# A hybrid decoder step: six query tiles multiplied as three pairs, decoding moved behind them

## What is computed

```python
def split_projection(h, w_in):
    z = jnp.einsum('bsd,de->bse', h, w_in)
    ...
    qd, kd, vd, gd, qw, kw, vw, gw, qm, gm = jnp.split(z, cuts, axis=-1)
    qd = qd.reshape(B, S, H_DIFF, 2, DK_DIFF)
...
    od = diff_attn_prompt(qd, kd, vd, lam, slopes_diff)
    ow = dilated_prompt(qw, kw, vw, slopes_dil)
    om = memory_attn(qm, mk, mv)
    yp = yp + gated_merge(od, gd, ow, gw, om, gm, g_subln[l], lam_init, w_out[l], yp.dtype)
...
    od = diff_attn_sample(qd, kd, vd, cache_k_diff[l], cache_v_diff[l], page_table, lam, slopes_diff)
```

## Time and profile before

| | |
|---|---|
| median of 3 runs | 1026.35 us (1026.08 to 1027.72) |
| the profiled execution's own time | 1026.25 us |
| its span, first to last instruction | 1024.5 us |
| PE busy | 1000.5 us, 98% |
| DVE busy | 723.7 us, 71% |
| ACT busy | 441.5 us, 43% |
| mean granted clock of TensorE | 0.997 of full speed |

### The profile page before, as it was taken

One profiled execution on the slowest core, in us unless ns is written; L12 is line 12 of the kernel. 1 busy time (PEld: TensorE's weight loads), 2 busy tenths in 40 slices (PEclk: granted clock), 3 DMA queues, 4 the chain that ended last, 5 costly groups with the idle time before them and its releaser, 6 DMA issues.

```text
span 1024.5 us, 24055 instructions
## 1 busy us (share of the span) xinstructions
PE 1000.5 (98%) x8103; PEld 980.4 (96%) x8103; DVE 723.7 (71%) x2687; ACT 441.5 (43%) x1169; POOL 54.7 (5%) x122
## 2 busy tenths in 40 slices
PE   7999999999999999999999999999999999999995
PEld 6899999999999999999999999999999999999995
DVE  5783267777788867778777676577774786588874
ACT  5763222222333333444342553335565365545552
POOL 0200000000000000000000000000000100000002
PEclk9999999999999999999999999999999999999998
DMA  9863288987978877777866686999662425234424
GB/s 300 250 195 107 64 266 265 293 271 226 266 220 254 259 231 235 219 224 207 245 200 192 186 249 181 231 280 284 193 191 72 140 74 153 94 104 145 124 84 167
DMA packets 254521, 203.33 MB, mean 198 GB/s; under 512 B 12480, under 2 KB 207670, under 8 KB 253750
## 3 DMA queue, kind: packets, MB, share of 16 engines
q1 hardware_dynamic: 253934, 200.67, 65.7%
q10 hardware_dynamic: 464, 1.12, 0.3%
HBM read 189.98 MB, written 11.76 MB: 197 GB/s over the span
## 4 chain that ended last, share of the span: by engine, by line
PE 91%; DVE 2%; ACT 2%; issue 2%; SPq 1%; DMA 1%; POOL 0%; DVEq 0%; POOLq 0%; ACTq 0%
PE z L1097 71%; PE z L1123 8%; PE o_ps L1193 2%; PE s_ps L1156 2%; PE t_ps L1143 2%; PE t_ps L1183 1%; PE s_ps L1161 1%; DMA w_raw<-in_w_mem_kv_dram 1%; PE o_ps L1198 1%; PE o_ps L1202 1%; PE s_ps L1168 1%; PE o_ps L1242 1%; ACT w_hi L1351 1%; PE s_ps L1028 1%; SPq L828 1%
## 5 line engine op out<-in xcount | busy, mean ns | idle before, releaser
L1097 PE MATMUL z<-act_hi,w_hi 128*128 128x260 f32 (+1 forms) x2048 | 440.9, 291 | 2.4 <-DVE act_lo L1629 2.3
L1097 PE MATMUL z<-act_hi,w_lo 128*128 128x260 f32 (+1 forms) x2048 | 422.4, 283 | 0.0
L1097 PE MATMUL z<-act_lo,w_hi 128*128 128x260 f32 (+1 forms) x2048 | 421.6, 282 | 0.0
L1097 PEld LDWEIGHTS z<-act_hi,w_hi 128*128 128x128 f32 x2048 | 321.5, 189 | 7.9 <-issue 4.0
L1097 PEld LDWEIGHTS z<-act_lo,w_hi 128*128 128x128 f32 x2048 | 319.9, 188 | 0.0
L1097 PEld LDWEIGHTS z<-act_hi,w_lo 128*128 128x128 f32 x2048 | 319.5, 188 | 0.0
L1676 DVE TENSOR_TENSOR w_lo<-w_raw,w_hi 128x512 fp32r<-128x512 f32 x302 | 206.8, 687 | 132.5 <-ACT w_hi L1351 131.8
L1351 ACT ACTIVATE w_hi<-w_raw 128x512 fp32r<-128x512 f32 x302 | 186.4, 626 | 200.4 <-PE z L1097 173.2
L1865 DVE CUSTOM_DVE_ANT_0 pages<-pages,q_bc 128x128 f32<-128x128 f32 x640 | 144.2, 285 | 21.2 <-DMA pages<-in_cache_k_win_dram 13.5
L1894 DVE SCALAR_TENSOR_TENSOR v_acc<-pages,dec_a,v_acc 128x256 f32<-128x256 f32 x224 | 94.3, 478 | 1.7 <-DMA pages<-in_cache_v_diff_dram 1.5
L1473 ACT ACTIVATE probs<-probs,st_n 128x128 f32<-128x128 f32 (+3 forms) x48 | 26.8, 558 | 79.9 <-DVE st_n L1804 79.6
(11 more groups left out here) (236 smaller groups left out, 1121.8 us busy)
## 6 DMA issues: line engine op xcount, KB each, us to landing
w_raw<-in_w_in_dram SPq DMA_DIRECT2D x224, 256.0 KB, 4.5
pages<-in_cache_k_diff_dram SPq DMA_DIRECT2D x128, 256.0 KB, 4.7
pages<-in_cache_v_diff_dram SPq DMA_DIRECT2D x128, 256.0 KB, 3.6
w_raw<-in_w_out_dram SPq DMA_DIRECT2D x64, 256.0 KB, 2.8
w_raw<-in_w_mem_kv_dram SPq DMA_DIRECT2D x32, 256.0 KB, 6.1
cat<-in_x_prompt_dram SPq DMA_DIRECT2D x8, 1024.0 KB, 6.0
q_bc<-q_rows_dram SPq DMA_DIRECT2D x32, 256.0 KB, 6.7
pages<-in_cache_mem_k_dram SPq DMA_DIRECT2D x16, 256.0 KB, 6.4
```

Source lines behind the costliest of these rows:

```text
L1097: last = nc.tensor.matmul(zb[:, bank, 0:b - a], lhs[:, w], rhs[:, kt, a:b], start=(kt == 0 and m == 0), stop=(kt == KT - 1 and m == 2))
```

## The change

Of the eight `qd` tiles the first two stay single tiles (ops 32 to 39), and the other six become three pairs (ops 40 to 81). The operands T1 to T4 of the tokens are made for them in the same `arena` as those of the output pairs. For that the tokens are first added up again from their high and low parts (`token_sum`, 16 instructions of 128x520), then `operand_add` makes T1 to T4 (8 groups of four instructions of 128x260), then they are split (8 times 128x1040 on ACT and on DVE). Since `arena` also holds pages, bias tables and keys, decoding begins four slots after the last pair instead of after the fourth query tile, and ends four slots later than before (slot 256 and on); its 320 units are spread over fewer slots. The operand sums of the output pairs, of which six groups stood ahead of the output tiles, now all stand behind their start. The sample columns of all eight query tiles are kept by one instruction behind the pairs.

```diff
@@ units
-        paired = kind == "y" and c == 0 and FIRST_PAIRED <= e <= LAST_PAIRED
+        paired = kind == "qd" and e >= SINGLE_HEADS or kind == "y" and c == 0 and FIRST_PAIRED <= e <= LAST_PAIRED
@@
+Q_PAIRS = H - SINGLE_HEADS
+Q_END = START[PAIRS_OF_TILES[Q_PAIRS - 1]] + 14
@@
-T_ADDS = ((2, -11), (0, -10), (1, -9), (4, -8), (5, -7), (3, -4), (6, 1), (7, 1))
+T_ADDS = ((2, 1), (0, 1), (1, 2), (4, 2), (5, 3), (3, 3), (6, 4), (7, 4))
 T_SPLITS = ((2, 0), (1, 0), (2, 1), (1, 1), (3, 0), (3, 1), (4, 0), (4, 1))
-T_SPLIT_AT = (-4, 2, 2, 3, 4, 4, 6, 8)
+T_SPLIT_AT = (5, 6, 7, 8, 9, 10, 11, 12)
...
+X_SUM_AT = tuple(IN_START + 1 + j // 2 for j in range(HALF_KT))
+X_ADD_AT = tuple(IN_START + 4 + 5 * j // 8 for j in range(HALF_KT))
+X_SPLIT_AT = tuple(IN_START + t for t in (9, 9, 10, 10, 11, 12, 14, 16))
@@ plan
-    first, end = DONE[AT["qd", 1, 1]] + 4, DONE[AT["gw", 3, 0]] - 2
+    first, end = Q_END + 4, DONE[AT["gw", 3, 0]] + 2
@@ product
-                    if k == 0:
-                        pe.wait_ge(s_tlo, T_SPLITS.index((t, i)) + 1)
+                    if k in (0, Q_PAIRS):
+                        pe.wait_ge(s_tlo, len(T_SPLITS) * (k // Q_PAIRS) + T_SPLITS.index((t, i)) + 1)
@@ operand_hi
-                act.wait_ge(s_tadd, T_ADDED[half])
+                act.wait_ge(s_tadd, HALF_KT + T_ADDED[half] if again else HALF_KT)
@@ vector
+            def token_sum(j):
+
+                dve.wait_ge(s_plo, 3 * N_PREP)
+                dve.wait_ge(s_xsl, 1)
+                for i in range(2):
+                    kt = HALF_KT * i + j
+                    last = nc.vector.tensor_tensor(x_full[:, j, i, :], act_hi[:, kt, :].bitcast(F32), act_lo[:, kt, :].bitcast(F32), ALU.add)
+                last.then_inc(s_xfull, 1)
@@ gpsimd
+            def keep_first():
...
+                pool.wait_ge(s_lo, Q_END)
+                for c in range(2):
+                    wait_tile(pool, AT["qd", SINGLE_HEADS - 1, c])
+                    wait_tile(pool, AT["qd", H - 1, c])
+                nc.gpsimd.tensor_copy(q_s[:, 0:2 * H, :], cat_t[:, 0:2 * H, SAMPLE]).then_inc(s_keep, 2 * H)
```

More of the change, by code:

```diff
@@ L125 @@
 N_TILES = len(TILES)
-FIRST_IN = AT["qd", 0, 0]
+FIRST_IN = 2 * H
 FIRST_OUT = AT["y", 0, 0]
@@ L209, in raw_loads @@
             used[slot] += 1
-            loads.append((n, r, slot, used[slot], event, at + (1 if first >= IN_END else AHEAD + 1)))
+            loads.append((n, r, slot, used[slot], event, at + (1 if first >= IN_END or IN_START + 8 <= first < Q_END else AHEAD + 1)))
         free += gone
@@ L413, in plan @@
         put(max(fin0 + (0, 3, 5)[k], DONE[AT["gw", 3, 0]] + (0, 0, 1)[k]), "fin", k, 0.8)
[L414 removed]
+    assert STEPS[-1][3] + 3 < IN_END - 4 and fin0 + 5 < IN_END - 4
     for j, (kt, turn) in enumerate(T_ADDS):
[L416 removed]
+        put(X_SUM_AT[j], "T", ("sum", j))
+        put(X_ADD_AT[j], "T", ("add", j))
+        put(IN_END + turn, "T", ("add", HALF_KT + j))
     for j in range(len(T_SPLITS)):
[L418 removed]
+        put(X_SPLIT_AT[j], "T", ("split", j))
+        put(IN_END + T_SPLIT_AT[j], "T", ("split", len(T_SPLITS) + j))
     rank = {"ynat": 5.5, "norm": 8, "evac": 0, "part": 0, "sum": 0, "P": 1, "B": 2, "D": 3, "C": 4, "A": 5, "do": 7, "dk": 8, "dv": 8}
@@ L1709, in part_out @@
                 out = product_out(k, p)
+                below, above = slice(0, HALF), slice(HALF, TOK)
+                queries = k < Q_PAIRS
+                if queries:
+                    row1, row2 = (cat_t[:, cat_slot(*TILES[n]), :] for n in (first, second))
+                else:
+                    row1, row2 = tall[:, 0, :], tall[:, 1, :]
                 dve.wait_ge(s_quarter, START[u] + 2 * p + 2)
@@ L1712, in part_out @@
                     dve.wait_ge(s_pact, k + 1)
-                    wait_tall(dve, first)
-                    nc.vector.tensor_tensor(tall[:, 0, 0:HALF], out, c1, ALU.add).then_inc(s_pdve, 1)
+                    if not queries:
+                        wait_tall(dve, first)
+                    nc.vector.tensor_tensor(row1[:, below], out, c1, ALU.add).then_inc(s_pdve, 1)
                 if name == "U":
@@ L1723, in part_out @@
                     dve.wait_ge(s_pdve, 7 * k + 4)
-                    wait_tall(dve, second)
-                    nc.vector.tensor_tensor(tall[:, 1, HALF:TOK], out, U, ALU.add).then_inc(s_pdve, 1)
+                    if not queries:
+                        wait_tall(dve, second)
+                    nc.vector.tensor_tensor(row2[:, above], out, U, ALU.add).then_inc(s_pdve, 1)
                 if name == "C12":
-                    nc.vector.tensor_tensor(tall[:, 0, HALF:TOK], out, X, ALU.add).then_inc(s_pdve, 1)
+                    nc.vector.tensor_tensor(row1[:, above], out, X, ALU.add).then_inc(s_pdve, 1)
@@ L2111, in slot @@
                     elif kind == "T":
-                        (operand_add if what[0] == "add" else operand_lo)(what[1])
+                        {"sum": token_sum, "add": operand_add, "split": operand_lo}[what[0]](what[1])
                     elif kind == "A":
@@ L2219, in slot @@
                         y_rstd(what)
-                    elif kind == "evac" and TILES[what] in KEPT:
+                    elif kind == "evac" and TILES[what] in KEPT and DONE[what] > Q_END:
                         keep(what)
+                    elif (kind, what) == ("part", (Q_PAIRS - 1, "C21")):
+                        keep_first()
                     elif kind == "C" and STEPS[what][0] == "diff":
```

101 lines of the change are left out of this document (55 added, 46 removed).

## The result

The changed kernel took **1046.7 us** (median of 4 runs, 1045.22 to 1048.56); the kernel before, on the same chip, 1026.55 us. The ratio is 1.0195 (95% interval 1.0177 to 1.0214). The profiled spans are 1045.0 and 1024.5 us: 20.5 us more, where 7.9 were forecast.

What follows compares the result with a forecast made beforehand. PE, in flight 98% of the span, was taken to bound the kernel. Saving -8.65, first pair +13.0, bank waits +1.8 and +0.7, decoding +1.0 gave +7.9 us on 1026.25: forecast 1034 us, range 1030 to 1039.

Steps and rivals of the forecast that it cites:

- the saving of 8.65: Three query pairs on PE save 72 matmuls of 0.120 us against single tiles: 8.65 us less.
- the first pair: Ops 40 to 53: PE waits for DVE's late w_lo and operand splits; 13.0 us booked, bounds 11 and 14.5.
- its milestones on DVE: First pair: DVE reaches w_lo of op 41 at 98.4, of op 43 at 104.7, fourth operand split 113.8, w_lo of op 52 127.7.
- The bank wait at op 82: Tile behind the third pair waits for the seventh product's addition, behind a split on DVE: 1.8 us, bounds 1.0 and 1.9.
- the one at the first output pair: First output pair waits 1.2 us for ACT to empty its bank; 0.7 booked, bounds 0 and 1.2.
- the decoding term: 320 units in fewer slots add DVE work, mostly hidden by w_lo's slack: +1.0 us, between -1 and +3.
- The prediction's own sign of being wrong: Whole run: the prediction is wrong if, among other signs, waits behind 200 us sum to more than 6 us.
- The operand sums of the output pairs: nothing: Output stage: DVE's later operand sums are covered, so nothing is booked; at most 1.5 us if the cover is gone.
- The clock was a rival: First pair: clock falls to 1.2 GHz in PE's gaps before ops 43 and 44, about 1.5 us: 1036; chance 0.16.
- Decoding gets in the way: Differential heads' stage: DVE near 88% makes turns and gates late in every head, +4 to +5 us, 1038; chance 0.14.
- the forecast case: Whole kernel: the booked terms sum to +7.9 us, 1034 us, own range 1031 to 1037; chance 0.59.

Runs made afterwards that it cites:

- late-decoding run: Kernel before, single query tiles throughout, with only decoding and the output pairs' operand sums and splits moved later as in the change: 1035.13 us, 1.0084 of before.
- two measurements of the same edit: Fourth and fifth softmax parts of decoding group 0 one slot later: on the changed kernel 1040.67 us, on the late-decoding run 1030.74 us.
- two-pair runs: Changed kernel with two single heads and two query pairs: 1029.21 us; also with later softmax parts 1025.10; further, decoding ending four slots earlier 1026.06, or window softmax later 1024.58.

## Why the prediction was wrong

**What held.** The direction, the saving of 8.65, and the first pair: 13.0 booked, 13.9 measured (98.38 to 172.79 for three pairs of 20.16), its milestones on DVE within 0.3 us. Its waits for `w_lo` and `t_lo` sum to 10.0 us with a longest of 4.0, where the prediction named 12 to 13 and 4. The 3.9 us up to 13.9 are, as near as the rows tell, op 44 at the lower clock and the slow first matmuls behind each of nine waits (behind the wait of 0.31 us at op 42 the next two starts came after 0.59 and 0.23 us, where the pace is 0.12). Pairs two and three ran full. The bank wait at op 82 was 1.96 us for 1.8 booked; the one at the first output pair was 0.93, where the prediction had a wait of 1.2 and booked 0.7 of it.

**The step that failed is the decoding term**, "+1.0, between -1 and +3". I sized it by the mean load of DVE. That load rose by more than the 2 in 50 forecast and did no harm: through head 2 DVE is busy 67.90 us of 81.46 (348.07 to 429.53), before 62.22 of 82.36 (333.15 to 415.51), PE is in flight all the time in both, and the distance to before stays at 14.9 us through all six tiles. What cost 5.1 us is one slot. The sentence "what the trace cannot show is how often a unit more falls ahead of a turn that PE waits for" names the mechanism and then leaves it to a guess, although the changed order tells it: C 3, three key units and a softmax part in slot 130. The late-decoding run puts this term at 8 us by itself, 4.4 to 6 of it that slot (two measurements of the same edit) and 3.9 the dilated steps. The prediction's own sign of being wrong, waits behind 200 us of more than 6 us, came true: those of 0.25 us or more sum to 10.7 us there (3.1 before).

"The operand sums of the output pairs: nothing" held as a term. The output stage still cost 1.8 us more than forecast; the rows give `w_lo` waits of 0.2 and 0.3 us and 0.75 us at the first kept tile, whose bank now is one that an addition (line 1755) frees. With an even number of query pairs (the two-pair runs) this last wait is not in the trace.

**The clock was a rival and should have been a term.** I gave it 0.16 and 1.5 us, in the first pair alone, because the trace of before had no gap in its middle. It was low at three places. In the first pair, where the rival had it, it cost no time: op 44 took nearly twice as long (2.7 us) behind its gap of 4.0 us, but op 45 still waited 0.57 us for `t_lo` and started at 115.12, when DVE let it. The time went at the two other places, 1.5 us behind the gap at op 82, which the prediction had booked without it, and 1.5 us in slot 130, a gap that it had not. By the page that I cited (the Trainium skill, TensorE: Matmul & The Clock Gate, Part 1) an idle TensorE loses half its clock; the trace agrees, and it does so behind gaps as short as 2 us, at times. The 1036 of this rival is nearer than 1034, but for a reason that did not hold, and 10.7 us short.

**The rivals.** "Decoding gets in the way" is what happened, with 8 us in place of 4 to 5, and not by DVE's share: by a collision. It and the clock came on top of the forecast case, not in place of it. The range of 1030 to 1039 treated them as alternatives; had both been added to the sum, it would have been 1034 + 4 + 1.5 = 1039.5. With the sizes that the runs give (decoding 8 in place of 1, the clock behind its slot within it; the clock behind op 82 1.5; the first pair 0.9 more; the start 1.1 later; the output stage 1.8 more) it is 1034.1 + 7 + 1.5 + 0.9 + 1.1 + 1.8 = 1046.4. That this closes on 1046.7 proves little, since the terms behind the 7 are read off the very trace that they explain; the 8 us of decoding are measured on another kernel.

**What stays open**: which of ACT's rounding and DVE's work holds the last 4 us of the first pair when the token sums are gone; why a sooner start was given back at 252 and 280 us; and the 0.5 to 1.6 us for which PE waits near 700 us for `probs` in every kernel whose decoding ends late (with the earlier end it is gone).

## What to carry to other kernels

When a change re-spreads jobs over slots, list each slot of the new order in which two jobs use one buffer and look at what stands between them on the engine that frees it; a mean load says nothing on that. Work that is done once for several short operations must fit ahead of them: add its instructions up against the room beside the long ones, and if it does not fit, take one short operation fewer. Price the gaps on TensorE with the clock that may fall behind them (here in 6 of 6 traces behind 3.2 us and in 3 of 5 behind 2.0 us, 1.5 us in most), unless another engine sets the pace there anyway, and read such a stretch by instruction counts, not by busy time.

## What the runs showed of the hardware

**The clock behind gaps.** The gap of 3.2 us in front of line 1249 (or its like) stood in six traces, and in all six the granted clock was low behind it, for 1.3 to 2.8 us of work lost. The gap of 2.0 us at op 82 stood in five traces: the clock fell in three and stayed full in two, with the same work of PE ahead of it and behind it. Behind the gap of 0.85 us in the two kernels that had it there it never fell. Once, in the run with two pairs, it was low behind a gap of 1.33 us; behind the gaps of 1.28 to 1.59 us near 700 us, in six traces, it was not. The one time:

```profile
720.00:724.00 4.00, 2.67 (x23) 2.47 (x21) 2.08 (x6) 1.55 (x4) 0.00 (x0) 1.00 1.02 335
724.00:728.00 4.00, 4.00 (x26) 4.00 (x25) 3.12 (x10) 0.89 (x3) 0.00 (x0) 0.68 0.76 256
```

So a profile of one execution can over- or understate such a gap by 1.5 us; part of the spread of these kernels (1026.51 to 1032.85 us for the two pairs) may be this, which is not shown.

**GpSimd and VectorE.** Instructions of 0.42 us lasted 1.43 to 1.56 us while GpSimd read and wrote the same kind of memory, about the length of one GpSimd instruction (1.50). The Trainium skill (SBUF — State Buffer, SBUF: two separate sides) says that the two share a pair of ports which one instruction holds to its end, also against a VectorE instruction with two inputs from SBUF; the trace agrees, and a GpSimd that looks idle is no free helper for a busy VectorE.
